# Wide column sums, idle matmuls and a new order in the second feed-forward norm and the final norm

## The reference

```python
y = token_mixer(...)                       # ends in "@ w_out"
x = x + g1 * rms_norm(y, post_mix_g)       # norm 4
h = rms_norm(x, pre_ffn_g) * (1 + sc2) + sh2   # norm 5
y = conv_ffn(h, w_up, conv_w, conv_b, w_down)
x = x + g2 * rms_norm(y, post_ffn_g)       # norm 6, the output
```

## Time and profile before

| | |
|---|---|
| median of 3 runs | 1814.29 us (1810.85 to 1821.24) |
| profiled execution | 1820.35 us, its span 1818.5 us |
| TensorE matmul (PE) busy | 1690.3 us, 93% of the span |
| TensorE weight load (PEld) busy | 1392.0 us, 77% |
| VectorE (DVE) / ScalarE (ACT) / GpSimd (POOL) busy | 879.5 us (48%) / 641.3 us (35%) / 810.5 us (45%) |
| mean granted TensorE clock | 0.960 of full |
| the crossing with norms 4 and 5 | about 1385 to 1432 us |
| output of norm 6 | about 1792 to 1818.5 us |

### The profile page before, as it was taken

One profiled execution on the slowest core, in us unless ns is written; L12 is line 12 of the kernel. 1 busy time (PEld: TensorE's weight loads), 2 busy tenths in 40 slices (PEclk: granted clock), 3 DMA queues, 4 the chain that ended last, 5 costly groups with the idle time before them and its releaser, 6 DMA issues.

```text
span 1818.5 us, 21748 instructions
## 1 busy us (share of the span) xinstructions
PE 1690.3 (93%) x8044; PEld 1392.0 (77%) x8044; DVE 879.5 (48%) x1225; ACT 641.3 (35%) x883; POOL 810.5 (45%) x664
## 2 busy tenths in 40 slices
PE   3998999999989999899999999899878899999996
PEld 1677778787768887788888888678667778888885
DVE  5546454555485353544336535574666355113423
ACT  3433434343223322432133223355144343334421
POOL 1273546545355554544444544232255345444442
PEclk7898999999999999999999999989988799999998
DMA  8111112121225435244555531211011132222221
GB/s 321 47 70 47 70 70 93 50 90 70 93 79 192 174 123 197 94 138 168 186 179 185 189 137 65 76 70 47 24 47 70 59 135 94 85 104 95 95 87 61
DMA packets 36391, 194.39 MB, mean 107 GB/s; under 512 B 4032, under 2 KB 6336, under 8 KB 20928
## 3 DMA queue, kind: packets, MB, share of 16 engines
q1 hardware_dynamic: 24768, 151.06, 23.0%
q10 hardware_dynamic: 11520, 41.95, 6.6%
HBM read 190.90 MB, written 2.10 MB: 106 GB/s over the span
## 4 chain that ended last, share of the span: by engine, by line
PE 72%; DVE 13%; POOL 6%; ACT 4%; issue 3%; DMA 2%; DVEq 0%; SPq 0%; ACTq 0%; POOLq 0%
PE main L821 52%; PE main L817 8%; POOL w_lo L632 5%; PE main L814 2%; ACT w_hi L1239 2%; PE main L873 1%; PE auxB L948 1%; DVE tmp L1904 1%; PE auxD L1027 1%; DMA ada_first<-w_ada 1%; PE auxD L1092 1%; DVE tmp L2303 1%; DMA x<-x_in 1%; PE auxC L1020 1%; PE auxB L1014 1%
## 5 line engine op out<-in xcount | busy, mean ns | idle before, releaser
L632 POOL TENSOR_TENSOR w_lo<-raw,w_hi 128x512 fp32r<-128x512 f32 (+1 forms) x522 | 698.6, 1369 | 808.8 <-ACT w_hi L1239 808.6
L821 PE MATMUL main<-h_hi,w_hi 128*128 128x512 f32 (+1 forms) x1088 | 435.9, 401 | 19.4 <-POOL w_lo L632 14.8
L821 PE MATMUL main<-h_lo,w_hi 128*128 128x512 f32 (+1 forms) x1088 | 429.9, 395 | 0.0
L821 PE MATMUL main<-h_hi,w_lo 128*128 128x512 f32 (+1 forms) x1088 | 429.6, 395 | 0.0
L1239 ACT ACTIVATE w_hi<-raw 128x2048 fp32r<-128x2048 f32 (+3 forms) x136 | 248.0, 1823 | 250.0 <-PE main L821 182.2
L821 PEld LDWEIGHTS main<-h_hi,w_hi 128*128 128x128 f32 (+1 forms) x1088 | 206.4, 190 | 75.5 <-POOL w_lo L632 22.6
L821 PEld LDWEIGHTS main<-h_hi,w_lo 128*128 128x128 f32 (+1 forms) x1088 | 206.3, 190 | 46.5 <-issue 1.0
L821 PEld LDWEIGHTS main<-h_lo,w_hi 128*128 128x128 f32 (+1 forms) x1088 | 206.7, 190 | 42.4 <-issue 0.2
L1904 DVE SCALAR_TENSOR_TENSOR tmp<-main,par,tmp 128x511 f32<-128x511 f32 x88 | 65.9, 749 | 176.7 <-ACT tmp L1340 174.9
L1929 DVE SCALAR_TENSOR_TENSOR ada_acc<-ada_raw,cs,ada_acc 128x1024 f32<-128x1024 f32 x70 | 116.7, 1667 | 40.5 <-DMA ada_raw<-w_ada 31.5
L817 PE MATMUL main<-w_hi,h_hi 128*128 128x512 f32 x224 | 91.8, 410 | 4.5 <-POOL w_lo L632 4.5
(11 more groups left out here) (465 smaller groups left out, 2724.7 us busy)
## 6 DMA issues: line engine op xcount, KB each, us to landing
raw<-stream SPq DMA_DIRECT2D x118, 1024.0 KB, 4.8
ada_raw<-w_ada ACTq DMA_DIRECT2D x80, 512.0 KB, 4.7
ada_first<-w_ada SPq DMA_DIRECT2D x16, 512.0 KB, 6.7
raw<-stream SPq DMA_DIRECT2D x8, 768.0 KB, 4.2
raw<-stream SPq DMA_DIRECT2D x8, 640.0 KB, 3.9
x<-x_in SPq DMA_DIRECT2D x2, 2048.0 KB, 10.1
out<-x SPq DMA_DIRECT2D x16, 128.0 KB, 1.8
con<-consts SPq DMA_DIRECT2D x1, 486.0 KB, 4.2
```

The source lines that it names most:

```text
L632: ins = nc.gpsimd.tensor_tensor(w_lo[:, s, a:b], raw[:, s, a:b], w_hi[:, s, a:b], ALU.subtract)
L821: ins = nc.tensor.matmul(bank[0:n, :], w[:, k, col:col + n], a[:, ka_, :], start=start, stop=stop)
```

## The change

Column sums (`column_sums` in all crossings, `square_columns` in `cross5`) move all 128 columns of ones instead of one; each writes 128 equal PSUM columns, of which ScalarE's root reads one for each group of tokens (`first_columns`). `idle` adds matmuls of the identity with itself into a free `main` bank: 4, 2 and 3 in `cross5`, 4 in `cross6`.

In `cross5` TensorE spreads the first reciprocal after tile 0 of job 3 and no longer after tile 2, and takes up the second half's sums between the first squares. Three `square_columns` of the second half run ahead of `behind_norm`, five inside its tiles 0 to 4, and the spread of the second half follows tile 4. ScalarE squares both last half tiles at once, ahead of `square_z`, and makes the high part of the next weights in four pieces. VectorE adds the squares earlier, and makes the norm-5 reciprocals after all products of norm 4 and before the last low part. Both sweeps keep their products in two free `main` banks and `aux` C, in turn (`sweep_bank`).

In `cross6` the last two evictions and the square addition of the second half lie inside the first half's output. The last square is not added to the others on VectorE: TensorE accumulates it (`last_columns`). GpSimd adds five tiles of eight (`BY_POOL`), VectorE three (`BY_DVE`), in the order `OUT_ORDER`, in which SyncE sends them too.

```diff
@@ -522,6 +522,9 @@
 acc4, squares = qk[:, 0, :], qk[:, 1:5, :]
+OUT_ORDER = (1, 3, 0, 5, 7, 2, 6, 4)
+BY_DVE = (0, 2, 4)
+BY_POOL = tuple(k for k in OUT_ORDER if k not in BY_DVE)
 half_cols = (slice(0, SEQ // 2), slice(SEQ // 2, SEQ))
@@ -532,6 +535,15 @@
 def sweep_slot(h, k):
     return aux["CDA"[k % 3]][:, 0:SEQ // 2] if h else tmp[:, 2 + k % 2, half_cols[(k // 2) % 2]]
+def sweep_bank(h, k):
+    j = units[unit_at["WO"][3]].job0
+    return (main[(j + 2) % 4], main[(j + 3) % 4], aux["C"])[(KD * h + k) % 3][:, 0:SEQ // 2]
+def first_columns(bank, h):
+    return bank[:, :].rearrange("p (c t) -> p c t", c=TC)[:, 2 * h:2 * h + 2, 0]
 def low_made(i, h, k):
@@ -551,7 +563,9 @@
 def added(k, h):
-    return (x_pool, 2 * KD + KD // 2 * h + k // 2 + 1) if k % 2 else (x_ready, 4 * KD + KD // 2 * h + k // 2 + 1)
+    if k in BY_POOL:
+        return x_pool, 2 * KD + len(BY_POOL) * h + BY_POOL.index(k) + 1
+    return x_ready, 4 * KD + len(BY_DVE) * h + BY_DVE.index(k) + 1
@@ -607,7 +621,7 @@
     for h in range(2):
-        for k in range(KD):
+        for k in OUT_ORDER:
             sp.wait_ge(*added(k, h))
@@ -725,8 +739,8 @@
     def cross6():
         for h in range(2):
-            for k in range(1, KD, 2):
-                pool.wait_ge(z_mul, 2 * KD + KD // 2 * h + k // 2 + 1)
+            for n, k in enumerate(BY_POOL):
+                pool.wait_ge(z_mul, 2 * KD + len(BY_POOL) * h + n + 1)
                 add_residual(k, h)
@@ -835,7 +849,7 @@
         for c in (2 * h, 2 * h + 1):
-            ins = nc.tensor.matmul(bank[:, c:c + 1], sums[:, chunk(c)], ones[:, 0:1], start=True, stop=True)
+            ins = nc.tensor.matmul(bank[:, chunk(c)], sums[:, chunk(c)], ones, start=True, stop=True)
         ins.then_inc(full, 1)
     def spread(i, h):
@@ -846,7 +860,12 @@
-    def behind_norm(u, i, h, at_k):
+    def idle(u, n):
+        for _ in range(n):
+            nc.tensor.matmul(main[u.job0 % 4][:, 0:P], ident, ident, start=True, stop=True)
+    def behind_norm(u, i, h, at_k, within_k={}):
@@ -860,6 +879,8 @@
                 if a is h_lo:
+                    if k in within_k:
+                        within_k[k]()
                     pe.wait_ge(*low_made(i, h, k))
@@ -884,8 +905,8 @@
         for c in (2 * h, 2 * h + 1):
-            ins = nc.tensor.matmul(aux[b][:, c:c + 1], squares[:, k // 2, half_cols[k % 2]][:, P * (c % 2):P * (c % 2 + 1)],
-                                   ones[:, 0:1], start=(k == 0 and c == 2 * h), stop=(k == KD - 1 and c == 2 * h + 1))
+            ins = nc.tensor.matmul(aux[b][:, chunk(c)], squares[:, k // 2, half_cols[k % 2]][:, P * (c % 2):P * (c % 2 + 1)],
+                                   ones, start=(k == 0 and c == 2 * h), stop=(k == KD - 1 and c == 2 * h + 1))
         if k == KD - 1:
@@ -894,16 +915,22 @@
         run(end[u.n])
-        project(u, 1, ((2, 3), {(2, 6): lambda: column_sums(4, 0), (3, 2): lambda: spread(4, 0)}))
-        for k in range(KD):
+        project(u, 1, ((2, 3), {(2, 6): lambda: column_sums(4, 0), (3, 0): lambda: spread(4, 0)}))
+        pe.wait_ge(main_free[v.job0 % 4], v.job0 // 4)
+        idle(v, 4)
+        square_columns(0, 0)
+        column_sums(4, 1)
+        square_columns(0, 1)
+        idle(v, 2)
+        spread(4, 1)
+        for k in range(2, KD):
             square_columns(0, k)
-            if k == 3:
-                column_sums(4, 1)
-            if k == 5:
-                spread(4, 1)
+        idle(v, 3)
         spread(5, 0)
-        behind_norm(v, 5, 0, {k: (lambda k=k: square_columns(1, k)) for k in range(KD)})
-        spread(5, 1)
+        for k in range(3):
+            square_columns(1, k)
+        within = {k: (lambda k=k: square_columns(1, k + 3)) for k in range(KD - 3)}
+        behind_norm(v, 5, 0, {KD - 4: lambda: spread(5, 1)}, within)
         behind_norm(v, 5, 1, {})
     def cross6(u):
@@ -912,8 +939,21 @@
         project(u, 1, ((2, 3), {(2, 4): lambda: column_sums(6, 0), (3, 1): lambda: spread(6, 0)}))
-        column_sums(6, 1)
+        last_columns(u)
         spread(6, 1)
+    def last_columns(u):
+        pe.wait_ge(main_free[u.job0 % 4], u.job0 // 4 + 1)
+        idle(u, 4)
+        bank, full = take(("cross", 6), 2)
+        pe.wait_ge(norm_add, (KD - 1) * (SPREAD.index(6) + 1) - 1)
+        for c in (2, 3):
+            nc.tensor.matmul(bank[:, chunk(c)], rstd[:, chunk(c)], ones, start=(c == 2), stop=False)
+        pe.wait_ge(norm_sq, squared(6) + KD)
+        for c in (2, 3):
+            ins = nc.tensor.matmul(bank[:, chunk(c)], tmp[:, (KD - 1) % 2, chunk(c)], ones, start=False, stop=(c == 3))
+        ins.then_inc(full, 1)
     def sum3(i, n):
@@ -1237,6 +1277,17 @@
         run_act(w_hi[:, s, 0:k], raw[:, s, 0:k], ACT.Copy).then_inc(hi_done, 1)
+    def split_quarter(u, a):
+        s = u.n % 2
+        q = u.kn * u.cols // 4
+        if a == 0:
+            act.wait_ge(raw_in[s], 16 * (u.n // 2 + 1))
+            act.wait_ge(*units_over(u.n - 1))
+        ins = run_act(w_hi[:, s, q * a:q * (a + 1)], raw[:, s, q * a:q * (a + 1)], ACT.Copy)
+        if a == 3:
+            ins.then_inc(hi_done, 1)
     def convolve(u, t):
@@ -1409,12 +1460,12 @@
     def root_half_of(i, h, b):
...
         c = slice(2 * h, 2 * h + 2)
-        run_act(root[:, c], bank[:, c], ACT.Sqrt, bias=NORM_EPS_OF[i], scale=1.0 / D_MODEL).then_inc(rt_half, 1)
+        run_act(root[:, c], first_columns(bank, h), ACT.Sqrt, bias=NORM_EPS_OF[i], scale=1.0 / D_MODEL).then_inc(rt_half, 1)
         return free
     def high_of(i, k, h):
         act.wait_ge(*crossed(tmp_half, norm_tmp, i, h, k))
-        run_act(h_hi[:, k, half_cols[h]], sweep_slot(h, k), ACT.Identity,
+        run_act(h_hi[:, k, half_cols[h]], sweep_bank(h, k), ACT.Identity,
                 bias=mod_at(NORMS[i][2])[:, k:k + 1]).then_inc(hi_half if h == 0 else norm_hi, 1)
     def cross5(u, v):
@@ -1441,23 +1492,27 @@
         square4(KD - 2, 1)
+        square4(KD - 1, 1)
         for k in range(KD):
             square_z(k, 0)
-            if k == 2:
-                square4(KD - 1, 1)
-            if k == 5:
+            if k == 1:
                 free = root_half_of(4, 1, 2)
+                split_quarter(units[v.n + 1], 0)
+            if k == 3:
+                split_quarter(units[v.n + 1], 1)
         act.wait_ge(rt_half, 6)
...
         root_half_of(5, 0, 4)
-        j = u.job0 + 1
-        act.wait_ge(main_full[j % 4], j // 4 + 1)
+        for k in range(2):
+            square_z(k, 1)
+        split_quarter(units[v.n + 1], 2)
+        square_z(2, 1)
         for k in range(KD):
             high_of(5, k, 0)
-            square_z(k, 1)
+            if k + 3 < KD:
+                square_z(k + 3, 1)
         root_half_of(5, 1, 6)
-        split_hi(units[v.n + 1])
-        act.wait_ge(*units_over(v.n))
+        split_quarter(units[v.n + 1], 3)
         for k in range(KD):
@@ -2025,16 +2080,16 @@
                 spread[h] = full(("cross", 5), 2 * h + 5)
-            if k >= 3 + (h == 0):
-                dve.wait_ge(*low_made(5, h, k - 3 - (h == 0)))
-            ins = stt(sweep_slot(h, k), x[:, k, cols], scale[:, k:k + 1], spread[h][0][:, cols], ALU.mult, ALU.mult)
+            if k >= 3:
+                dve.wait_ge(*low_made(5, h, k - 3))
+            ins = stt(sweep_bank(h, k), x[:, k, cols], scale[:, k:k + 1], spread[h][0][:, cols], ALU.mult, ALU.mult)
             ins.then_inc(norm_tmp if h else tmp_half, 1)
         def low(k, h):
...
             dve.wait_ge(*crossed(tmp_half, norm_tmp, 5, h, k))
-            stt(h_lo[:, k, cols], sweep_slot(h, k), shift[:, k:k + 1], h_hi[:, k, cols], ALU.add,
+            stt(h_lo[:, k, cols], sweep_bank(h, k), shift[:, k:k + 1], h_hi[:, k, cols], ALU.add,
                 ALU.subtract).then_inc(lo_half if h == 0 else norm_lo, 1)
         def z_products(h, ks):
@@ -2055,23 +2110,24 @@
         invert_of(4, 0)
+        add_square_of(4, KD - 2, 1)
         dve.wait_ge(ysum_ready, Y_AT[4] - 2)
-        z_products(0, range(KD))
-        add_square_of(4, KD - 2, 1)
+        z_products(0, range(4))
         add_square_of(4, KD - 1, 1)
+        z_products(0, range(4, 6))
         invert_of(4, 1)
-        z_products(1, range(3))
+        z_products(0, range(6, KD))
+        z_products(1, range(KD))
         invert_of(5, 0)
-        z_products(1, range(3, KD))
         dve.wait_ge(x_pool, KD)
...
             if k >= 2:
+                if k - 2 == KD - 1:
+                    invert_of(5, 1)
                 low(k - 2, 0)
-        invert_of(5, 1)
         dve.wait_ge(lo_half, 2 * KD)
-        dve.wait_ge(*units_over(v.n))
         for k in range(KD + 2):
@@ -2090,12 +2146,12 @@
-        def output(h):
+        def output(h, ks):
             cols = half_cols[h]
             r, free = full(("cross", 6), 2 * h + 1)
-            for k in (1, 0, 3, 2, 5, 4, 7, 6):
+            for k in ks:
                 ins = scale_y(5, k, h, r)
-                if k % 2:
+                if k in BY_POOL:
                     ins.then_inc(z_mul, 1)
```

(23 more changed lines are left out.)

## The result

The changed kernel has a median of 1794.8 us (1789.57 to 1797.7, four runs) beside 1815.49 us (1810.85 to 1821.24, four runs) for the kernel before. The ratio is 0.9875 with a 95% interval of 0.9854 to 0.9895. The forecast was 1792.5 us in a range of 1785 to 1802; the medians differ by 20.7 us, and the steps had added up to 21.7. Run again beside eleven runs of the kernel before, it came out at 1791.4 against 1815.72 us, ratio 0.9863 (0.9835 to 0.9892).

A forecast was written before the change was run, and what follows sets the result against it. TensorE, at 93% of the span, bounds the kernel, losing time to waits and half clock; VectorE sets the end. Gains of 15.8 and 5.9 us sum to 21.7, giving 1792.5 us from the 1814.29 median, range 1785 to 1802.

The forecast's parts named there:

- Steps 1 and 3: Second feed-forward norm: 128-column sums cost 0 us at full clock, and with idle matmuls the full clock holds.
- The rival built on it: Norm: if idle gaps alone decide, wide sums change nothing and the clock falls again; about 1797 us, 22%.
- Step 2: Idle matmuls in the norm, 1.2, 0.6 and 0.9 us, fill TensorE's waits; taken as 0 us of delay.
- Steps 4 and 5: Norm's second-half products start at 1396.2, not 1398.69; first sweep at 1400.4, not 1402.9: 2.5 us earlier.
- Step 6: Norm's first sweep in three PSUM banks, not four SBUF slots: costs 0.1 us, at most 0.6.
- Steps 7 and 8: Next unit's first half ends at 1410.3, not 1421.3; second sweep and half at 1416.2, not 1432.00: gain 15.8 us.
- the new wait for the spread: In the next unit's first half, the spread behind the fifth tile waits for the root: about 0.4 us.
- Rival B: Norm: clock held but statistics not earlier, first sweep still at 1402.9, all behind it 2.5 us later: 1795 us, 10%.
- rival A: Norm: clock falls again and returns during the next unit's first half, costing about 4.5 us: 1797 us, 22%.
- Step 9: Next weights split in four pieces: about 2.1 us of ScalarE for 1.9; the 3.48 us stall moves along unchanged.
- Step 10: Kernel's end: VectorE's waits fall inside the first output, GpSimd takes five adds; last add at 1809.9, not 1815.86: 5.9 us.

The follow-up runs named there:

- filled sums: Changed kernel with one-column sums again, two idle 128-column matmuls behind each pair in the norm: 1804.12 us, ratio 0.9923 against the kernel before.

## Why the prediction was right

**Steps 1 and 3, wide sums and clock: right, and shown.** Four records of 128 columns take 0.44 us from start to start at full clock, those of one column too. One-column sums put back cost 10.8 us of the norm in the profile, and about 0.5% of the time. The reading of the rows had one slip: no spread lies in the five microseconds before the fall, the next one starts at 1397.45, just behind it. And step 1 gave the wide sums of the earlier crossings a cost of 0 to 0.1 us and no gain; the profile has 2.8 us less in the crossing with norm 2. *The Trainium skill (TensorE: Matmul & The Clock Gate, Why this matters for your kernels) warns of idle gaps. The rival built on it would have had the wide sums do nothing. Here gaps of 1.45 and 1.73 us kept 2.4 GHz with wide sums, and one-column sums lost it 3.6 us behind a gap of 0.57. That gaps also cost something is seen in the kernel with the wide sums alone: waits of 2.67 and 1.34 us, and a fall of 3.4 us at each.*

**Step 2, idle matmuls: cost nothing, as said, and bring nothing.** The prediction held the clock "with 1 and 2". Only 1 was needed; this part of the reason was wrong, without effect on the number.

**Steps 4 and 5, statistics earlier: right, a little late.** Counted from the first sums, the second half's products start at 8.63 us (forecast 8.2), the first sweep at 13.2 (forecast 12.4, before 14.9). The gain is 1.7 us in place of 2.5. The reciprocal of norm 5 is at 1390.21, 0.24 us behind the last product, and the sweep's first product 0.8 behind its spread, where I had 0.7.

**Step 6, the sweep in PSUM: no cost.** In SBUF slots it gives the same time, within the intervals. The two products that the prediction compared, 0.468 and 0.489 us, both read the spread from PSUM and differ in where they write. The low parts differ in where they read, and took 0.471 us from SBUF and 0.477 from PSUM before:

```profile
L2037 DVE SCALAR_TENSOR_TENSOR h_lo<-auxC,mod,h_hi x3: 476/477/478, 1424.6 to 1429.6; 128x256 fp32r<-128x256 f32 x3
```

*The rule of the Trainium skill on VectorE's fixed part (VectorE: DVE Perf Modes, TRN2 errata) was priced at 1 us over the sweep; neither the page's price nor the trace's reached TensorE, which takes 1.16 us a tile there where VectorE takes 0.91.*

**Steps 7 and 8: the term that was off.** First half 9.1 us (forecast 8.8), the new wait for the spread 0.41 (forecast 0.4). The second half takes 6.2 us where I had 5.8 to 5.9: TensorE catches up with the second sweep, whose last low part starts at 1406.22. Together with the sweep's 0.8 the norm ends at 29.6 us and not 28: the gain is 14.4, not 15.8. Rival B (sweep as late as before) had 2.5 us of delay, and 0.8 came; rival A (the clock falls in the norm) did not come in any of the seven profiled executions with wide sums and the new order (six kernels, the changed one twice).

**Step 9, the split in quarters: right.** The stall moved along as 3.48 us. That little can be had from it was not in the prediction: taken away, it came back as 2.19 us a unit later.

**Step 10, the end: right.** 5.9 us in the profile, 6.3 by the medians with the end alone; VectorE's longest wait between is under 0.3 us; GpSimd's five adds do not bind.

**The sum: right, with some luck.** 21.7 forecast, 20.7 and 24.3 measured. Of the two terms the profile gives 20.3: the norm has 1.4 less than forecast, the end what was forecast. Two parts that were in no step stand against this, 1.0 between and behind the two and 2.8 in the crossing with norm 2. The parts alone add up to 8.5 (wide sums) and 6.3 (end) of the 20.7 to 24.3 us between the medians; the rest I put down to the new order in the norm, which takes away the waits of 2.67 and 1.34 us and the two falls behind them: 35.9 to 29.6 us. That the order does this was not tried by itself without wide sums and the end; the kernel with one-column sums has it and still has a norm of 40.4, 3.6 shorter than before.

## What to carry to other kernels

When TensorE's granted clock falls at a place where it is busy, look at how wide its matmuls are and not at its gaps alone. Here a reduction over the partitions moved 128 columns in the time of one, 0.44 us a pair from start to start at full clock, and with the new order that kept the clock; an added dummy matmul costs its own time where TensorE does not wait. A wait that is removed pays only if what is next in line is not as late: here the first wait came back as TensorE's own work, and the weight stall in large part a unit later.

## What the runs showed of the hardware

One-column sums also bear on the short falls. The same first wait, 1.73 to 1.75 us, was followed by a fall of 3.4 us in three of five profiled kernels whose first sums had one column (with one-column sums put back, with idle matmuls alone, and with filled sums; not in the kernel before, nor with the end alone), and in none of the six that had it with 128 columns. The fall in the crossing with norm 2 came in all five profiled executions with one-column sums and in one of eight with wide ones, behind a wait of 2.09 us that both forms have. These are single executions, and a fall at one place can be chance.

With one-column sums put back, the clock stayed at 1.2 GHz from 1396.0 to 1419.9 although TensorE was busy 0.99 or more in every microsecond of it. With wide sums between the tiles (the wide sums alone) it was back 3.4 us after the fall. What exactly the chip counts, these runs do not say.
